# A mixture-of-experts kernel: where the spare row blocks go between the experts

## The reference, cut to what matters

```python
g_sel = argmax(softmax(h @ w_group) + b_group)          # one of 4 groups
e_prob = softmax((h @ w_expert)[group g_sel])           # 8 experts in the group
top_idx = top_k(e_prob + e_bias, 2)                     # 2 experts for each token
y[token] = sum over the 2: weight * (silu(x @ w_gate[e]) * (x @ w_up[e])) @ w_down[e]
```

## Time and profile before

| | us |
|---|---|
| median of 3 runs | 2265.36 |
| lowest and highest | 2262.91, 2268.09 |
| span of the profiled execution, first to last instruction | 2263.9 |
| first expert stage, from the first transpose of gathered rows to the last scatter | 1082 to 1578 |
| second expert stage | 1746 to 2241 |

### The profile page before, as it was taken

One profiled execution on the slowest core, in us unless ns is written; L12 is line 12 of the kernel. 1 busy time (PEld: TensorE's weight loads), 2 busy tenths in 40 slices (PEclk: granted clock), 3 DMA queues, 4 the chain that ended last, 5 costly groups with the idle time before them and its releaser, 6 DMA issues.

```text
span 2263.9 us, 30578 instructions
## 1 busy us (share of the span) xinstructions
PE 1953.3 (86%) x9801; PEld 1085.4 (48%) x9802; DVE 805.5 (36%) x1896; ACT 669.2 (30%) x1058; POOL 84.9 (4%) x105
## 2 busy tenths in 40 slices
PE   8899999999899999998886887877897967777885
PEld 4534777745467775654332333333774423333332
DVE  2273333312433335445332333333224423323334
ACT  1142100012410002142543444443202533434443
POOL 2000000000000000000000000000000000000000
PEclk9889999999999999999897998998997988988998
DMA  8574434433934443314799999996655999999993
GB/s 279 217 293 169 141 139 166 177 149 150 414 114 161 143 167 130 149 38 172 305 421 377 381 403 410 390 421 261 269 186 211 368 421 388 420 421 377 413 393 157
DMA packets 84026, 609.20 MB, mean 269 GB/s; under 512 B 16224, under 2 KB 16544, under 8 KB 21744
## 3 DMA queue, kind: packets, MB, share of 16 engines
q1 hardware_dynamic: 72368, 595.03, 66.6%
q0 software_dynamic: 10720, 11.05, 1.4%
q10 hardware_dynamic: 864, 2.19, 0.2%
HBM read 613.45 MB, written 19.92 MB: 280 GB/s over the span
## 4 chain that ended last, share of the span: by engine, by line
PE 68%; DMA 19%; DVE 4%; issue 3%; ACT 3%; DVEq 2%; SPq 1%; ACTq 0%; POOLq 0%
PE ps L837 26%; PE ps L1230 14%; PE ps L1083 13%; DMA big<-in_w_up 8%; PE ps L1095 6%; DMA big<-in_w_down 5%; DMA big<-in_w_gate 5%; PE ps L1232 3%; PE ps L851 3%; ACT big L1711 2%; DVEq L2434 1%; DVE hT L2442 1%; PE ps L1259 1%; DMA c_res<-f_rows,big 1%; PE ps L1222 1%
## 5 line engine op out<-in xcount | busy, mean ns | idle before, releaser
L1230 PE MATMUL ps<-big,hT 128*32 128x512 f32 x3072 | 721.1, 625 | 150.7 <-ACT big L1711 150.1
L1232 PE MATMUL ps<-big,hT 128*32 x1536 | 719.8, 625 | 0.0
L1711 ACT COPY big<-big 128x1024 f32 x384 | 395.0, 1046 | 528.9 <-DVEq L2414 263.1
L2421 DVE TENSOR_SCALAR big<-big 128x1024 f32 x384 | 262.9, 696 | 626.3 <-PE ps L1232 381.8
L1230 PEld LDWEIGHTS ps<-big,hT 128*32 128x32 f32 x3072 | 200.0, 114 | 545.4 <-DVE big L2421 283.2
L1083 PE MATMUL ps<-hT,big 128*128 128x256 f32 x1408 | 311.1, 379 | 0.0
L837 PE MATMUL ps<-big,hT 128*128 128x512 f32 (+4 forms) x792 | 297.9, 534 | 5.6 <-ACT hT L1646 3.3
L1083 PEld LDWEIGHTS ps<-hT,big 128*128 128x128 f32 x1408 | 267.2, 190 | 52.4 <-issue 18.2
L837 PEld LDWEIGHTS ps<-big,hT 128*128 128x128 f32 x792 | 143.2, 193 | 149.5 <-issue 140.1
L837 PE MATMUL ps<-big 64*30 64x256 f32 (+14 forms) x704 | 148.6, 483 | 29.0 <-DVE big L2371 8.1
L1232 PEld LDWEIGHTS ps<-big,hT 128*32 128x32 f32 x1536 | 164.2, 114 | 5.6
(11 more groups left out here) (332 smaller groups left out, 1169.5 us busy)
## 6 DMA issues: line engine op xcount, KB each, us to landing
big<-in_w_down SPq DMA_DIRECT2D x128, 1024.0 KB, 17.0
big<-in_w_gate SPq DMA_DIRECT2D x128, 1024.0 KB, 11.9
big<-in_w_up SPq DMA_DIRECT2D x128, 1024.0 KB, 12.4
big<-in_dense SPq DMA_DIRECT2D x45, 2048.0 KB, 7.8
big<-in_dense SPq DMA_DIRECT2D x52, 1536.0 KB, 6.6
big<-in_dense SPq DMA_DIRECT2D x5, 1024.0 KB
big<-y_rows SPq DMA_DIRECT2D x4, 1024.0 KB, 6.5
f_rows<-big ACTq DMA_DIRECT2D x4, 512.0 KB, 8.6
```

The costliest lines, as they stand in the source:

```text
L1230: nc.tensor.matmul(ps[g * SLOTS:(g + 1) * SLOTS, bank, :], xT[:, k, g * SLOTS:(g + 1) * SLOTS], side[:, g - 1, quarter % 2, at:at + BW], s ...
L1232: return nc.tensor.matmul(ps[0:SLOTS, bank, :], xT[:, k, 0:SLOTS], experts3[:, bass.ds(here, 1), kind * CH + row:kind * CH + row + BW] .re ...
L1711: nc.scalar.copy(side[:, 1, quarter % 2, :], experts3[:, bass.ds(there, 1), lo:lo + QW] .rearrange("p a n -> p (a n)")).then_inc(s["side2_ ...
L2421: ts(side[:, 0, quarter % 2, :], experts3[:, bass.ds(there, 1), lo:lo + QW].rearrange("p a n -> p (a n)"), 1.0, None, mult).then_inc(s["si ...
```

## The change

The spare blocks (48 less the blocks needed) are placed in another way. Before, the begin of expert e is moved by e/32 of them, rounded down. After, expert e begins at block 1.5 e (rounded down) or behind it, as long as there are spare blocks: with C(e) the blocks of the experts ahead, the shift is min(spare, max over j up to e of (floor(1.5 j) - C(j))), not below zero. The maximum up to each expert is made in five doubling steps on VectorE over two buffers (`lead`), whose first 16 columns are zero. The end of an expert is read out of `pst` itself with a one-hot product and a sum, ahead of the wait for TensorE's seventh signal; before, it was worked out from three small products of TensorE's, which go. The router's constants change to match. Numbers of blocks and rounds, the loads and their order, and the work of a round stay.

```diff
--- before.py
+++ after.py
@@ -150,8 +150,9 @@
     e = np.arange(E)
     r = np.zeros((P, 4, E), f)
     r[:E, 0] = e[:, None] < e[None, :]
-    r[:, 1] = e
-    r[:, 2] = (np.arange(P) + 1)[:, None]
+    r[:, 1] = WIDE * e // 2
+    r[np.arange(E - 1), 2, e[1:]] = 1.0
+    r[E - 1, 2, E - 1] = 2 * NB
     r[:E, 3, 0] = (e + 1) % BPE - e % BPE
     for q in range(BPE):
         r[:E, 3, 1 + q] = 16.0 * ((e + 1) % BPE == q)
@@ -410,8 +411,10 @@
         eqB = area(RB + 1448, 4, ROUNDS)
         onB = area(RB + 1528, 4, 3, ROUNDS)
         nbT = area(RB + 1768, P)
-        rest = area(RB + 1896, E + 1)
-        pad_i = area(RB + 1929, E + 1).bitcast(i32)
+        SHIFTS = tuple(1 << i for i in range(E.bit_length() - 1))
+        lead = area(RB + 2680, 2, SHIFTS[-1] + E)
+        rest = area(RB + 2776, 1)
+        next_at = area(RB + 1896, E)
         pst = area(RB + 1962, E)
         pend = area(RB + 1994, 1)
         past = area(RB + 1995, NB)
@@ -574,7 +577,7 @@
             st["ent" + tag] = Stage(squares_done=2 * T, rvar_done=T, rstd_done=T, rstd_ready=T, turn_ready=2 * T,
                                     turned_a=2 * T, z_done=1, zdiag_done=1, z_ready=2, z_copied=2,
                                     f_stored=16 * T)
-            st["route" + tag] = Stage(aux_loaded=64, route_pe=9, route_dve=9, route_act=1)
+            st["route" + tag] = Stage(aux_loaded=64, route_pe=8, route_dve=9, route_act=1)
             st["moe" + tag] = Stage(
                 rows_gathered=16 * nb, xT_ready=2 * nb, xT_done=2 * nb, side1_copied=12 * nb, side2_copied=12 * nb,
                 half_landed=6 * nb, quarter_done=12 * nb,
@@ -1192,9 +1195,6 @@
                 mm(ps[:, 3, 0:E], nbT[0:E, :], rt[0:E, 0, :], True, True)
                 mm(ps[:, 3, E:2 * E], nbT[0:E, :], const["ones"][0:E, 0:E], True, True, s["route_pe"].sem)
                 pe.wait_ge(e["z_copied"].sem, e["z_copied"].end)
-                mm(ps[0:E, 4, 0:1], rt[0:E, 0, :], nbT[0:E, 0:1], True, False)
-                mm(ps[0:E, 4, 0:1], const["ident"][0:E, 0:E], nbT[0:E, 0:1], False, True)
-                mm(ps[0:E, 4, 1:2], const["ones"][0:E, 0:E], nbT[0:E, 0:1], True, True, s["route_pe"].sem)
                 pe.wait_ge(s["route_dve"].sem, s["route_dve"].at(6))
                 pe.wait_ge(g2["act_evac"].sem, g2["act_evac"].end)
                 for q in range(2 * TC):
@@ -2245,6 +2245,7 @@
                 tt(wrG, wr, gsm[:].unsqueeze(2).broadcast_to([P, KT, G + E]), mult)
                 link(v, tt(swK, wr, mod[:, layer, 3 * KT:4 * KT, 0].unsqueeze(2).broadcast_to([P, KT, G + E]), mult))
                 nc.vector.tensor_reduce(swS, swK.rearrange("p k n -> p n k"), AX.X, add).then_inc(r["route_dve"].sem, 1)
+                nc.vector.memset(lead[:, :, 0:SHIFTS[-1]], 0.0)
                 nc.vector.tensor_copy(vals[:, :, 1], const["tokid"][:])
                 for k in range(2):
                     nc.vector.tensor_copy(vals[:, k * TC:(k + 1) * TC, 0], const["tokid"][:, 0:TC])
@@ -2350,10 +2351,13 @@
                 L(ins)
 
                 v.wait_ge(s["route_pe"].sem, s["route_pe"].at(6))
-                L(ts(rest[:, 0:E], ps[:, 3, E:2 * E], -1.0, float(NB), mult, add))
-                L(tt(pad_i[:, 0:E], rest[:, 0:E], rt[:, 1, :], mult))
-                L(ts(pad_i[:, 0:E], pad_i[:, 0:E], E.bit_length() - 1, None, ALU.logical_shift_right))
-                L(tt(pst, ps[:, 3, 0:E], pad_i[:, 0:E], add))
+                first = SHIFTS[-1]
+                ts(rest, ps[:, 3, E:E + 1], -1.0, float(NB), mult, add)
+                L(tt(lead[:, 0, first:], rt[:, 1, :], ps[:, 3, 0:E], sub))
+                for i, n in enumerate(SHIFTS):
+                    old, new = lead[:, i % 2, :], lead[:, 1 - i % 2, :]
+                    L(tt(new[:, first:], old[:, first:], old[:, first - n:first - n + E], ALU.max))
+                L(stt(pst, lead[:, len(SHIFTS) % 2, first:], rest, ps[:, 3, 0:E], ALU.min, add))
                 before = ps[:, 1, 0:TC * E].rearrange("p (t n) -> p t n", t=TC)
                 L(stt(rank, pst.unsqueeze(1).broadcast_to([P, TC, E]), float(SLOTS), before, mult, add))
                 for k in range(2):
@@ -2371,19 +2375,16 @@
                     ins = tt(onB[:, :, x, :], eqB, wide(vals[:, :, x], ROUNDS), mult)
                 ins.then_inc(step, 1)
 
+                L(nc.vector.tensor_tensor_reduce(out=next_at[0:E, :], in0=pst[0:E, :], in1=rt[0:E, 2, :], scale=1.0,
+                                                 scalar=0.0, op0=mult, op1=add, accum_out=pend[0:E, :]))
+                ts(past[0:E, :], const["iota"][0:E, 0:NB], pend[0:E, :], None, ALU.is_ge).then_inc(step, 1)
                 v.wait_ge(s["route_pe"].sem, s["route_pe"].at(7))
-                L(ts(rest[0:E, E:E + 1], ps[0:E, 4, 1:2], -1.0, float(NB), mult, add))
-                L(tt(pad_i[0:E, E:E + 1], rest[0:E, E:E + 1], rt[0:E, 2, 0:1], mult))
-                L(ts(pad_i[0:E, E:E + 1], pad_i[0:E, E:E + 1], E.bit_length() - 1, None, ALU.logical_shift_right))
-                L(tt(pend[0:E, :], ps[0:E, 4, 0:1], pad_i[0:E, E:E + 1], add))
-                ts(past[0:E, :], const["iota"][0:E, 0:NB], pend[0:E, :], None, ALU.is_ge).then_inc(step, 1)
-                v.wait_ge(s["route_pe"].sem, s["route_pe"].at(8))
                 nc.vector.tensor_copy(slot_w, ps[:, 6, 2 * ROUNDS:3 * ROUNDS])
                 ts(slot_i, ps[:, 6, 0:2 * ROUNDS].rearrange("p (a b) -> p a b", a=2), FAR, None, add).then_inc(step, 1)
                 L(ts(need_i[:, 0:E - 1], pst[0:1, 1:E], -1.0, 171.0, add, mult))
                 L(ts(need_i[:, 0:E - 1], need_i[:, 0:E - 1], 9, None, ALU.logical_shift_right))
                 L(ts(need_i[:, 0:E - 1], need_i[:, 0:E - 1], 12.0, 2.0, mult, add))
-                v.wait_ge(s["route_pe"].sem, s["route_pe"].at(9))
+                v.wait_ge(s["route_pe"].sem, s["route_pe"].at(8))
                 nc.vector.tensor_copy(tab_i, ps[0:1, 5, 0:256].rearrange("p (a b) -> p a b", a=4)[:, :, 0:NB])\
                     .then_inc(step, 1)
 
```

## The result

The changed kernel ran at 2269.97 us, the median of 20 runs (2261.62 to 2278.40), the kernel before beside it at 2265.84 (20 runs, 2262.91 to 2270.15). The ratio is **1.0019** (95% interval 1.0010 to 1.0027): no gain, if anything 4 us lost, where 33.6 had been forecast. The profiled execution of the changed kernel spans 2270.2 us.

The account below looks back on a forecast made before the run. The prediction took weight transfers, with holes in their queue, to bound the expert stages. Its terms -15.5 - 14.1 - 5.5 + 1.5 gave -33.6 us; 2263.9 - 33.6 + 1.5 made 2232 us, range 2222 to 2248.

Parts of the forecast that it names:

- (a): First expert stage: 20.0 us lost in transfer holes mostly closes, less 3 and 1.5 that stay: -15.5 us.
- (b): Second expert stage: 15.6 us lost in transfer holes closes, less 1.5 that stays: -14.1 us.
- the 31.4 us round: Expert-stage round read as two experts' weights at 421 GB/s, 29.9 us, with row traffic and gaps making 31.4.
- The rounds and their experts: Both expert stages: rounds of three different experts fall from 8 to 1 and from 6 to none.
- round 13 14 15: First stage's remaining three-expert round: expert 16 waits for a slot, one short hold, 0 to 5.3 us, taken as 3.
- (c): End of the second stage: last round follows the last transfer by 14.6 us where it was 20.1, -5.5 us.
- (d): Routing's new vector steps on the path to the first gather: +0.75 us a layer, +1.5 in both.
- (e): Routing's other instructions: the new reduction is covered by VectorE's idle time, small products go; counted as nothing.
- TensorE the bound: Rival, expert stages: evenly spread idle time keeps TensorE's clock down, rounds take 34.0 us at 0.73; 2294 us, chance 0.04.
- The queue still held up: Rival, expert stages: slow TensorE releases slots late, smaller holes stay, half the hole gain left; 2247 us, chance 0.18.
- No more than their mean: Rival, expert stages: transfers give only their mean rate, holes close in appearance; 2261 us or no change, chance 0.06.

Follow-up runs that it names:

- Without rows: Either kernel with the second stage's gathers and scatters kept to row 0, so nearly no rows move: changed kernel 2235.60 us, kernel before 2245.54 us.
- the wider one: Changed kernel with row i of a block at place 8 (i mod 4) + i div 4: 2249.86 us, ratio 0.9924.
- the first spread kernel: Changed kernel with row i of a block at place 4 (i mod 8) + i div 8: 2236.98 us, run again 2237.40 us.

## Why the prediction was wrong

**The step that failed** is the size of (a) and (b): "The lost time is 444 x (1 - 402/421) = 20.0 us in the first stage and 439 x (1 - 406/421) = 15.6 us in the second. It sits in holes." All of the shortfall of the sum of 16 engines was taken for holes that the rounds dig. Part of it was engines waiting for the fullest one. Landings go at the pace of that one, and it was slower than 421 GB/s throughout; the holes closed and the mean stayed, 402 to 400 and 406 to 404. Without rows the second stage of the kernel before runs at 413 GB/s, by the same formula 420 x (1 - 413/421) = 8.0 us of holes, where (b) had counted 15.6. The same error sits in the reading of the 31.4 us round as "with row traffic and gaps": 29.9 us are the bytes, and by the count the 1.5 were the rows of the fullest engine, which the change then raised from 100 to 128. The placing did not only move waits, it moved rows onto the eight engines of blocks 0 and 1: nothing in the prediction asked which engine carries them, and no rival did.

The ledger of stage 1: placing -10.5 us (479.8 to 469.3, without rows), rows +11.7 (32.4 against 20.7), together +1.2, which is what the lengths show (500.5 to 501.7). Stage 0 was not run without rows; with rows spread in both kernels the placing is worth 3.2 us there and 4.7 in stage 1.

**Part by part.** *The rounds and their experts* came as worked out; the holes of the earlier trace rows are gone but for the one of round 13 14 15. *(a)*, -15.5: measured, the stage is 0.6 us longer. The pause in round 13 14 15 was held to be short; it was 23.1 us, longer than before. *(b)*, -14.1: of it and (c) together -10.5 is real, without rows. *(c)*, -5.5: without rows the last half lands 17.1 us ahead of the last result with the old placing and 10.3 with the new, -6.8, so the term was sound; with rows it is 17.0 and 9.5, but all landings come later and nothing of it is left. *(d)*, +1.5: measured 2 x 0.80 = +1.6. *(e)*, nothing: right; the idle time ahead of the copy grew from 1.17 to 1.68 us.

**The rest of the 4 us.** The lengths give 0.6 + 1.2 and (d) 1.6, together 3.4; the medians differ by 4.1. The profiled executions differ by 6.3, of which 2.9 us are there when the first routing reaches the new steps (1070.19 against 1067.27); why is not known.

**The rivals.** *TensorE the bound* did not come: the clock in the stretches is 0.92 and 0.93, and the rounds wait for transfers. The two clock levels that the rivals reckoned with are in the trace of the kernel before: the round of 24.8 us ran at a granted clock of 1.00, the stretch 1194 to 1214 was granted 0.50, and the matmuls of L1232 follow each other there by 0.85 us (1209.53, 1210.38), where it is 0.43 from 1214.58 on (1215.01, 1215.44). *The queue still held up* did not come but for the one pause. *No more than their mean* named the outcome (2261 against 2270, and no change), though "for whatever reason in the memory" was not the reason: the engines do deliver 421 GB/s for 210 us on end (1330 to 1540). It had been given 0.06. The measured rate of 421 was used to argue against it, and that rate was not the one that landings go by.

## What to carry to other kernels

When transfers bound a stage, take the time from one landing to the next, or per unit of work, and not bytes over time: with 16 engines the mean rate can be full while every landing waits for the same engine (here 421 GB/s, rows included, and 16.18 us per expert where 14.94 would do). Small indirect transfers beside a weight stream are to be counted per engine, in packets (here 0.16 us for each row of 4096 bytes); which partitions hold the real rows decides it. Spreading them costs a few instructions (here 23 us gained in the kernel before and 33 in the changed one, for four comparisons in place of one), but a spread has to be checked against the engines that the places lie on: the wider one used half of them and gained less. Before a change of placement is priced, ask what else moves with it.

## What the runs showed of the hardware that I had not expected

- A 4096-byte row packet takes 0.16 us and delays the weight stream on its engine by that: rows of 2% of the bytes cost 32.4 us of 501.7.
- In a gather or scatter over 128 places, places 4k to 4k+3 share an engine with places 32+4k to 32+4k+3: inferred (from chains of eight and one for rows at 0 to 3 and 32 to 36, of eight and three for rows at 0 to 6 and 32 to 35), and the count by this map is within 0.13 us of every time per expert in the table.
- Places that hold no row still make a packet of 4 bytes, of about 9 ns (4752 packets on queue 0 from 1700 to 2260, with rows and without): without rows the stage ran at 15.02 us per expert against 14.94 from the full rate.
- The DMA engines of one core moved 421 GB/s for 210 us on end, and 420 for 410 us without rows.
- A half took 25.28 us from issue to landing, so transfers of about that long were in flight, an estimate; in the first spread kernel a pause of SyncE's queue at expert 16 of stage 0 (1261.07 to 1290.02, 28.9 us for four halves) did not show in the landings: four took 11.1 us there, elsewhere 9.9 to 12.1.
